# VectorE adds the scaled residual of four sublayers to the product, in place of TensorE matmuls with a scaled identity

## The chip, the cores and the metric

The kernel runs on one core of a Trainium2 chip (trn2). The metric is the device time of one execution in microseconds (us); lower is better.

## The reference

The reference is two transformer blocks over 256 tokens of width 1024, in fp32. Seven sublayers matter here, numbered 1 to 7 as `b` in the code.

```python
for i in range(DEPTH):                     # DEPTH = 2, ALPHA = (2 * DEPTH) ** 0.25
    y = mixer_i(x)                         # i = 0: short convolution, i = 1: latent attention
    x = _layer_norm(ALPHA * x + y, ln_mix_g[i], ln_mix_b[i])
    x = _layer_norm(ALPHA * x + _sq_relu_mlp(x, ff_w1[i], ff_w2[i]), ln_ff_g[i], ln_ff_b[i])
# second block
x = x + 0.5 * swiglu(rms_norm(x, ...))
x = x + hybrid_mixer(x, ...)
x = x + 0.5 * swiglu(rms_norm(x, ...))
return rms_norm(x, final_norm)
```

Sublayers 1 to 4 are the two mixers and the two MLPs of the first block: each ends in a product `y`, a residual `ALPHA * x`, and a layer norm. Sublayers 5 to 7 belong to the second block, add the residual with a factor of 0.5 or 1, and are followed by an RMS norm.

## The kernel before

**Tiling.** Tokens stand on the 128 partitions in two tiles (`TILES`), so `x_tok` is [128, 2, 1024]. Each tile is handled in two halves of 512 columns (`HALVES`). The accumulator `acc` is PSUM, [128, 4, 512]: bank `2 * tile + h` holds half `h` of tile `tile` of a sublayer's product. Four more PSUM banks, `up[0..3]`, take the products into the hidden width, the transposes and the filler matmuls.

**Weights.** SyncE loads the weights in slabs of up to 1 MB into a ring of four (`raw`). ScalarE rounds each slab to `weight_hi` (L569) and VectorE takes the rest, `weight_lo` (L933). Every product is three matmuls: high by high, high by low, low by high (L1401 to L1403 into `up`, L1434, L1435 and L1437 into `acc`).

**The end of a sublayer.** `last_products` finishes tile 0 of `acc` first, then the two halves of tile 1, and signals `acc_part` and `slab_used`. VectorE's `layer_norm` (called for b = 1 to 4) then does for each tile: statistics of both halves from `acc` (L983), their aggregation (L985), subtract and scale by the gain from `acc` into `x_tok` (L992), and multiply by the root and add the bias in `x_tok` (L997). GpSimd works out the root in between (L487, L488). The residual is already in `acc` by then.

**How the residual got there.** `carry` starts each accumulator bank with a matmul of `x_tok` by `alpha_ident`, ALPHA times the identity, in fp32 (L1507, 512 columns each; each leaves two records in the trace). Four are issued for every one of the sublayers 1 to 4: at the start of the program for the first, two in `turn` and two in `mlp_part` for each MLP, and one after each of the steps 1 to 4 of the attention for the third. For sublayers 5 and 7 the accumulator is started with `clear_acc` instead, four matmuls of a single row of zeros (L1513).

**The next sublayer's operand.** `turn` is TensorE's code between two sublayers: fillers (`keep_warm`, bf16 matmuls of zeros, L1478), transposes of tile 0 (`turn_tile`, L1489), `carry` of tile 0, fillers, transposes of tile 1. Each half of a tile is transposed when its `tok` signal comes. ScalarE copies the transposes to `xh` (L569) and VectorE takes the rest to `xl` (L933). `WARM` holds the numbers of fillers: 9 and 8 for b = 1, 4 and 3 for b = 3, 22 and 0 for b = 4. Between sublayers 2 and 3, TensorE transposes tile 0, multiplies it by the first weights of the attention (`fresh_product`, L1620, L1621, L1626), and transposes tile 1 after that; VectorE there takes the rest of tile 0 (`middle`) between the statistics and L992 of tile 1. After sublayer 4 a second norm follows, the RMS norm of the second block (squares by ScalarE, L609, and L1015 by VectorE), before the transposes.

**Order.** Every engine's order is written out by hand and kept by semaphores; nothing is scheduled by a program. The first SyncE transfer brings the constants up to `C_ANTI`, the identity and the scaled identity, 128 KB.

Of the kernel before, what the change touches and what calls it, by code (L numbers as in the profile page):

```python
# [26 lines left out]
ALU = mybir.AluOpType  # L27
AX_X = mybir.AxisListType.X

P = 128  # L30
# [4 lines left out]
HALF = 512  # L35
# [7 lines left out]
ALPHA = (2.0 * DEPTH) ** 0.25  # L43
# [25 lines left out]
ROWS = ROW_XBC_B + XT  # L69


C_ID, C_ALPHA, C_ANTI, C_TRI, C_AFTER, C_SWAP, C_COS, C_SIN = 0, 128, 256, 384, 512, 640, 768, 1024
C_ALL = 1280


def shape_constants():

    c = np.zeros((P, C_ALL), np.float32)
    i = np.arange(P)
    c[:, C_ID:C_ID + P] = np.eye(P)  # L80
    c[:, C_ALPHA:C_ALPHA + P] = ALPHA * np.eye(P)
    c[:, C_ANTI:C_ANTI + P] = np.eye(P)[::-1]
    c[:, C_TRI:C_TRI + P] = i[:, None] <= i[None, :]
    c[:, C_AFTER:C_AFTER + P] = i[:, None] > i[None, :]

    h = ROPE // 2
    for d in range(P):
        src, sign = (d + h, -1.0) if d % ROPE < h else (d - h, 1.0)
        c[src, C_SWAP + d] = sign
    inv = np.float32(10000.0) ** (-np.arange(0, ROPE, 2, dtype=np.float32) / np.float32(ROPE))  # L90
    ang = np.arange(TOKENS, dtype=np.float32)[None, :] * inv[i % h][:, None]
    c[:, C_COS:C_COS + TOKENS] = np.cos(ang)
    c[:, C_SIN:C_SIN + TOKENS] = np.sin(ang)
    return c


def two_blocks(nc, t, consts, out):
# [40 lines left out]
    with ExitStack() as ctx:  # L138
# [10 lines left out]
        x_tok = sb("x_tok", [P, TILES, D])  # L149
# [9 lines left out]
        gain = sb("gain", [P, D])  # L159
        bias = sb("bias", [P, D])  # L160
        gain2 = sb("gain2", [P, D])
        cst = sb("cst", [P, C_ALL])
        rows = sb("rows", [ROWS, P])
# [5 lines left out]
        stat = sb("stat", [P, TILES, 2, 6])  # L169
        mean_var = sb("mean_var", [P, TILES, 2])  # L170
        rstd = sb("rstd", [P, 4])
# [5 lines left out]
        acc = ctx.enter_context(nc.psum_tensor("acc", [P, 4, HALF], F32))  # L177
        up = [ctx.enter_context(nc.psum_tensor(f"up{i}", [P, HALF], F32)) for i in range(4)]

        ident = cst[:, C_ID:C_ID + P]  # L180
        alpha_ident = cst[:, C_ALPHA:C_ALPHA + P]
        anti = cst[:, C_ANTI:C_ANTI + P]
        tri = cst[:, C_TRI:C_TRI + P]
        after = cst[:, C_AFTER:C_AFTER + P]
# [71 lines left out]
                return self.s[n]  # L256

        NORMS = 8
        norm = [Sems(f"norm{b}", "rows rstd tok" + " stat" * (b <= 4) + " resid squares" * (b >= 4)) if b else None for b in range(NORMS)]

        turned, operand_high, operand_low, acc_part = (
            sem("turned"), sem("operand_high"), sem("operand_low"), sem("acc_part"))
# [658 lines left out]
        def _(dve):  # L921
            steps = [0]
            vec = nc.vector

            def then(ins):

                steps[0] += 1
                ins.then_inc(dve_step, 1)
                dve.wait_ge(dve_step, steps[0])
# [43 lines left out]
            HALVES = (slice(0, HALF), slice(HALF, D))  # L973

            def layer_norm(b, last, rows_landed, ready, middle=None):

                for tile in range(TILES):
                    x = x_tok[:, tile, :]  # L980
                    for h, c in enumerate(HALVES):
                        product_done(b, tile, h, last)
                        ins = vec.bn_stats(stat[:, tile, h, :], acc[:, 2 * tile + h, :])  # L983
                    then(ins)
                    vec.bn_aggr(mean_var[:, tile, :], stat[:, tile, :, :].rearrange("p a b -> p (a b)"))\  # L985
                        .then_inc(norm[b]["stat"], 1)
                    if tile and middle:
                        middle()
                    dve.wait_ge(norm[b]["rows"], rows_landed)
                    dve.wait_ge(norm[b]["stat"], tile + 1)  # L990
                    for h, c in enumerate(HALVES):
                        ins = vec.scalar_tensor_tensor(x[:, c], acc[:, 2 * tile + h, :], mean_var[:, tile, 0:1], gain[:, c],  # L992
                                                       ALU.subtract, ALU.mult)
                    then(ins)
                    dve.wait_ge(norm[b]["rstd"], tile + 1)
                    for c in HALVES:
                        vec.scalar_tensor_tensor(x[:, c], x[:, c], rstd[:, tile:tile + 1], bias[:, c],  # L997
                                                 ALU.mult, ALU.add).then_inc(norm[b][ready], 1)
# [242 lines left out]
            for tile in range(TILES):  # L1241
                sl = slice(tile * SSD_HEADS, (tile + 1) * SSD_HEADS)
                ins = vec.tensor_tensor(x_dt[:, sl], acc[:, 2, sl], dtb_row, ALU.add)
# [144 lines left out]
        def _(pe):  # L1388
            mm = nc.tensor.matmul
# [102 lines left out]
            def turn(b, src):  # L1492
                if b:
                    keep_warm(WARM[b][0])
                turn_tile(b, src, 0)
                if b in (1, 3):
                    carry(0)
                if b:
                    keep_warm(WARM[b][1])
                turn_tile(b, src, 1)  # L1500
                if b in (4, 6):
                    clear_acc()

            def carry(tile, halves=(0, 1)):

                for h in halves:
                    mm(acc[:, 2 * tile + h, :], alpha_ident, x_tok[:, tile, h * HALF:(h + 1) * HALF], start=True,  # L1507
                       stop=False, skip_group_check=True)

            def clear_acc():  # L1510

                for n in range(4):
                    mm(acc[:, n, :], zeros[0:1, 0:P], zeros[0:1, :], start=True, stop=False, skip_group_check=True)  # L1513
# [5 lines left out]
            keep_warm(8)  # L1519
            pe.wait_ge(ident_landed, 16)  # L1520
            turn(0, x_tok)
            carry(0)
            carry(1)


            m = S_SC
# [27 lines left out]
            def mlp_part(i, b):  # L1554
                s, q = S_FF[i], mlp[i]
                weights(s)
                carry(1, (0,))
                up_product(s, up[0], b - 1)
                carry(1, (1,))
                with pe.Fori(0, FF_CHUNKS // 2 - 1) as it:  # L1560
                    for j in range(4):
                        m = s + 1 + j
                        weights(m, 4 * it)
                        if j % 2 == 0:
                            up_product(m, up[(1, 0)[j // 2]])
                        else:
                            pe.wait_ge(q["chunk"], 2 * it + (1 + j // 2))
                            down_product(m, *hidden(j // 2), CT)
                m = s + N_FF - 3
                weights(m)  # L1570
                up_product(m, up[1])
                last_products(b, CT, [(m + 1, *hidden(0), lambda: pe.wait_ge(q["chunk"], FF_CHUNKS - 1)),
                                      (m + 2, *hidden(1), lambda: pe.wait_ge(q["chunk"], FF_CHUNKS))])
# [193 lines left out]
                down_product(WO + c, *latent_rows(c), CT)  # L1767

            for g in range(HEADS + 1):
                if g == 1:  # L1770
                    step(g, values_ready)
                elif g in (6, 7):
                    step(g, lambda: first_rows(g - 6))
                else:
                    step(g)
                if 1 <= g <= 4:
                    carry((g - 1) // 2, ((g - 1) % 2,))
            last_products(3, CT, [(WO + c, *latent_rows(c), lambda c=c: heads_out(c)) for c in (2, 3)])

            turn(3, x_tok)  # L1780
# [181 lines left out]
```

## Time and profile before

| | |
|---|---|
| median of 3 runs | 1182.96 us (1181.51 to 1185.43) |
| span of the profiled execution | 1181.9 us (its own run time is not listed apart from the three) |
| PE (TensorE matmul) busy | 1162.1 us, 98% |
| PEld (TensorE weight load) busy | 1041.8 us |
| DVE (VectorE) busy | 658.0 us, 56% |
| ACT (ScalarE) busy | 514.1 us, 43% |
| POOL (GpSimd) busy | 51.0 us, 4% |
| mean granted TensorE clock | 0.993 |

A profile is one execution. Its times are in us, durations marked ns are the mean of one instruction. The chain of waits follows the work that ended last back through whatever released it. "PEclk" is the clock that TensorE was granted, 1.00 for 2.4 GHz and 0.50 for 1.2 GHz.

### The profile page before, as it was taken

Reading aid. Unit: us, or ns where it says so; the run is one execution under the profiler, and the core shown is the slowest. Engines: PE = TensorE matmul, PEld = TensorE weight load, DVE = VectorE, ACT = ScalarE, POOL = GpSimd, SP = SyncE. Lnnn points to the kernel's source line nnn. Section 1 sums busy time; section 2 is a strip of 40 time slices with the busy share of each in tenths; the row PEclk is TensorE's granted clock in tenths of the full one; section 3 lists DMA queues with packets and bytes.
Section 4 is the critical chain, followed back from the end, with each engine's and each line's share of the span. In section 5 each row is a group of like instructions: output and inputs, shape, how many; then the busy total and the mean of one; then the engine's idle time right before and its main releaser. Section 6 shows DMA issues by size and latency. Waiting matters only on the chain.

```text
span 1181.9 us, 18506 instructions
## 1 busy us (share of the span) xinstructions
PE 1162.1 (98%) x7660; PEld 1041.8 (88%) x7668; DVE 658.0 (56%) x717; ACT 514.1 (43%) x581; POOL 51.0 (4%) x93
## 2 busy tenths in 40 slices
PE   9999999999999999999999999999999999999997
PEld 7997999998977799999889999989988878999996
DVE  4757554555654755545654544467854565544543
ACT  4433444443544344444344443445635644434342
POOL 1000000000200100000000000010120010000000
PEclk9999999999999999999999999998989999999999
DMA  9664656554641565565346555556651144456541
GB/s 338 220 211 146 213 178 197 182 180 120 211 161 36 177 219 179 190 183 187 127 144 213 178 177 177 198 156 202 192 164 37 37 161 139 149 181 206 189 148 54
DMA packets 140908, 199.67 MB, mean 169 GB/s; under 512 B 9240, under 2 KB 119024, under 8 KB 140864
## 3 DMA queue, kind: packets, MB, share of 16 engines
q1 hardware_dynamic: 138160, 190.27, 50.0%
q0 software_dynamic: 2704, 8.79, 2.4%
q8 instruction: 32, 0.52, 0.2%
q14 instruction: 12, 0.10, 0.0%
HBM read 197.99 MB, written 1.05 MB: 168 GB/s over the span
## 4 chain that ended last, share of the span: by engine, by line
PE 92%; DVE 3%; ACT 2%; DMA 2%; POOL 1%; issue 1%; SPq 0%; DVEq 0%; POOLq 0%; ACTq 0%
PE up L1401 15%; PE up L1403 15%; PE up L1402 15%; PE acc L1434 11%; PE acc L1435 11%; PE acc L1437 11%; DMA raw<-in_sc_w_in 2%; PE acc L1507 1%; PE up L1489 1%; PE up L1850 1%; PE up L1876 1%; PE up L1478 1%; PE up L1873 1%; PE up L1743 1%; PE up L1423 1%; PE up L1427 1%
## 5 line engine op out<-in xcount | busy, mean ns | idle before, releaser
L933 DVE TENSOR_TENSOR weight_lo<-raw,weight_hi 128x2048 fp32r<-128x2048 f32 (+3 forms) x206 | 414.4, 2017 | 312.4 <-ACT weight_hi L569 312.2
L1401 PE MATMUL up<-xh,weight_hi 128*128 128x256 f32 x1548 | 441.3, 285 | 1.9 <-ACT cols L569 0.8
L569 ACT ACTIVATE weight_hi<-raw 128x2048 fp32r<-128x2048 f32 (+3 forms) x206 | 347.3, 1693 | 213.6 <-PE acc L1437 119.7
L1402 PE MATMUL up<-xl,weight_hi 128*128 128x256 f32 x1548 | 438.9, 283 | 0.0
L1403 PE MATMUL up<-xh,weight_lo 128*128 128x256 f32 x1548 | 438.8, 283 | 0.0
L1401 PEld LDWEIGHTS up<-xh,weight_hi 128*128 128x128 f32 x1548 | 297.8, 192 | 5.9 <-issue 1.7
L1402 PEld LDWEIGHTS up<-xl,weight_hi 128*128 128x128 f32 x1548 | 297.9, 192 | 2.7 <-issue 0.7
L1403 PEld LDWEIGHTS up<-xh,weight_lo 128*128 128x128 f32 x1548 | 297.7, 192 | 0.0
L1434 PE MATMUL acc<-weight_hi,hh 128*128 128x512 f32 x480 | 187.6, 391 | 0.6 <-DVE hl L933 0.4
L1435 PE MATMUL acc<-weight_lo,hh 128*128 128x512 f32 x480 | 187.5, 391 | 0.0
L1437 PE MATMUL acc<-weight_hi,hl 128*128 128x512 f32 x480 | 150.3, 389 | 0.0
L1437 PEld LDWEIGHTS acc<-weight_hi,hl 128*128 128x128 f32 x480 | 90.1, 188 | 19.1
L1434 PEld LDWEIGHTS acc<-weight_hi,hh 128*128 128x128 f32 x480 | 90.3, 188 | 18.8 <-issue 1.9
L1435 PEld LDWEIGHTS acc<-weight_lo,hh 128*128 128x128 f32 x480 | 90.3, 188 | 17.0
L656 ACT ACTIVATE tmp_a<-up 128x512 f32<-128x512 f32 x32 | 19.1, 598 | 120.7 <-PE up L1403 115.9
L1074 DVE TENSOR_TENSOR tmp_b<-tmp_a 128x512 f32<-128x512 f32 x32 | 22.2, 693 | 65.5 <-ACT tmp_a L656 65.5
L1434 PE MATMUL acc<-weight_hi,xh 128*128 128x256 f32 (+2 forms) x168 | 55.8, 332 | 1.3 <-DVE xl L933 1.3
L692 ACT ACTIVATE tmp_a<-up 128x512 f32<-128x512 f32 x22 | 13.1, 597 | 97.3 <-PE up L1403 93.2
L1435 PE MATMUL acc<-weight_lo,xh 128*128 128x256 f32 (+2 forms) x168 | 55.2, 329 | 0.0
L1437 PE MATMUL acc<-weight_hi,xl 128*128 128x256 f32 (+2 forms) x168 | 50.6, 328 | 0.0
L569 ACT ACTIVATE xh<-up 128x512 fp32r<-128x512 f32 (+1 forms) x43 | 22.7, 551 | 55.2 <-PE up L1489 43.0
L933 DVE TENSOR_TENSOR xl<-up,xh 128x512 fp32r<-128x512 f32 (+1 forms) x43 | 25.2, 629 | 27.5 <-ACT xh L569 27.3
(215 smaller groups left out, 892.7 us busy)
## 6 DMA issues: line engine op xcount, KB each, us to landing
raw<-in_ff_w SPq DMA_DIRECT2D x64, 1024.0 KB, 5.7
raw<-in_ffn_w_gate SPq DMA_DIRECT2D x22, 1024.0 KB, 5.3
raw<-in_ffn_w_up SPq DMA_DIRECT2D x22, 1024.0 KB, 5.4
raw<-in_ffn_w_down SPq DMA_DIRECT2D x44, 512.0 KB, 4.7
raw<-in_w_in SPq DMA_DIRECT2D x16, 1024.0 KB, 5.7
raw<-in_sc_w_in SPq DMA_DIRECT2D x11, 1024.0 KB, 7.3
raw<-in_w_out SPq DMA_DIRECT2D x6, 1024.0 KB, 5.0
raw<-in_sc_w_out SPq DMA_DIRECT2D x4, 1024.0 KB, 5.3
```

Of the source, the lines that this page charges most:

```text
L569: return nc.scalar.activation(dst, src, ACT.Copy, **kw)
L656: nc.scalar.activation(tmp_a[:, :], up[par][:, :], ACT.Relu).then_inc(q["relu"], 1)
L692: nc.scalar.activation(tmp_a[:, :], up[2 * par][:, :], ACT.Silu).then_inc(q["gate"], 1)
L933: return vec.tensor_tensor(dst, whole, high.bitcast(F32), ALU.subtract)
L1074: vec.tensor_tensor(tmp_b[:, :], tmp_a[:, :], tmp_a[:, :], ALU.mult).then_inc(q["squared"], 1)
L1401: mm(dst, w_h, xh[:, x_tile + k, :], start=first and k == 0, stop=False)
L1402: mm(dst, w_h, xl[:, x_tile + k, :], start=False, stop=False)
L1403: ins = mm(dst, w_l, xh[:, x_tile + k, :], start=False, stop=last and k == k_tiles - 1)
L1423: mm(dst, w_h[k], xh[:, k, :], start=k == 0, stop=False)
L1434: mm(d, s_h, h, start=first, stop=False, **open_group)
L1435: mm(d, s_h, l, start=False, stop=False, **open_group)
L1437: ins = mm(d, s_l, h, start=False, stop=last, **open_group)
```

## The change

TensorE no longer puts the residual into `acc`. All `carry` calls and the scaled identity are gone; `clear_acc` starts the banks in their place, once for each sublayer: at the start of the program, at the end of `turn` for b = 1 and 3, and before step 2 of the attention. VectorE's `layer_norm` first adds: for each half, `x_tok = ALPHA * x_tok + acc`, and then takes the statistics and the subtraction from `x_tok`. Two waits on VectorE's own sum precede the statistics. The constants shrink by 128 columns, all of them in the first transfer.

```diff
-C_ID, C_ALPHA, C_ANTI, C_TRI, C_AFTER, C_SWAP, C_COS, C_SIN = 0, 128, 256, 384, 512, 640, 768, 1024
-C_ALL = 1280
+C_ID, C_ANTI, C_TRI, C_AFTER, C_SWAP, C_COS, C_SIN = 0, 128, 256, 384, 512, 640, 896
+C_ALL = 1152
...
                     for h, c in enumerate(HALVES):
                         product_done(b, tile, h, last)
-                        ins = vec.bn_stats(stat[:, tile, h, :], acc[:, 2 * tile + h, :])
-                    then(ins)
+                        vec.scalar_tensor_tensor(x[:, c], x[:, c], ALPHA, acc[:, 2 * tile + h, :], ALU.mult, ALU.add)\
+                            .then_inc(norm[b]["sum"], 1)
+                        if h:
+                            dve.wait_ge(norm[b]["sum"], 2 * tile + 1)
+                            vec.bn_stats(stat[:, tile, 0, :], x[:, HALVES[0]])
+                    dve.wait_ge(norm[b]["sum"], 2 * tile + 2)
+                    then(vec.bn_stats(stat[:, tile, 1, :], x[:, HALVES[1]]))
...
-                        ins = vec.scalar_tensor_tensor(x[:, c], acc[:, 2 * tile + h, :], mean_var[:, tile, 0:1], gain[:, c],
+                        ins = vec.scalar_tensor_tensor(x[:, c], x[:, c], mean_var[:, tile, 0:1], gain[:, c],
...
                 turn_tile(b, src, 0)
-                if b in (1, 3):
-                    carry(0)
                 if b:
                     keep_warm(WARM[b][1])
                 turn_tile(b, src, 1)
-                if b in (4, 6):
+                if b in (1, 3, 4, 6):
                     clear_acc()
-
-            def carry(tile, halves=(0, 1)):
-
-                for h in halves:
-                    mm(acc[:, 2 * tile + h, :], alpha_ident, x_tok[:, tile, h * HALF:(h + 1) * HALF], start=True,
-                       stop=False, skip_group_check=True)
...
             turn(0, x_tok)
-            carry(0)
-            carry(1)
+            clear_acc()
...
                 weights(s)
-                carry(1, (0,))
                 up_product(s, up[0], b - 1)
-                carry(1, (1,))
...
             for g in range(HEADS + 1):
+                if g == 2:
+                    clear_acc()
...
                     step(g)
-                if 1 <= g <= 4:
-                    carry((g - 1) // 2, ((g - 1) % 2,))
```

The order of VectorE's instructions at the end of sublayer 1, before (tile 0, then the head of tile 1):

```order
L933 TENSOR_TENSOR weight_lo<-raw,weight_hi 128x2048
L983 BN_STATS stat<-acc 128x6 x2
L985 BN_AGGR mean_var<-stat 128x2
L992 SCALAR_TENSOR_TENSOR x_tok<-acc,mean_var,gain 128x512 x2
L997 SCALAR_TENSOR_TENSOR x_tok<-x_tok,rstd,bias 128x512 x2
```

And with the change:

```order
L931 TENSOR_TENSOR weight_lo<-raw,weight_hi 128x2048
L981 SCALAR_TENSOR_TENSOR x_tok<-x_tok,acc 128x512 x2
L985 BN_STATS stat<-x_tok 128x6
L987 BN_STATS stat<-x_tok 128x6
L988 BN_AGGR mean_var<-stat 128x2
L995 SCALAR_TENSOR_TENSOR x_tok<-x_tok,mean_var,gain 128x512 x2
L1000 SCALAR_TENSOR_TENSOR x_tok<-x_tok,rstd,bias 128x512 x2
```

Two instructions of 512 columns stand ahead of the statistics of each tile, and nothing has left VectorE. The same holds for both tiles of each of the four sublayers.

The order of TensorE's instructions between sublayers 1 and 2, before:

```order
L1437 MATMUL acc<-weight_hi,hl 128x512
L1478 MATMUL up<-zeros 128x512 x9
L1489 MATMUL up<-cst,x_tok 128x128 x8
L1507 MATMUL acc<-x_tok,cst 128x512 x2
L1478 MATMUL up<-zeros 128x512 x8
L1489 MATMUL up<-cst,x_tok 128x128 x8
L1507 MATMUL acc<-x_tok,cst 128x512
```

And with the change:

```order
L1440 MATMUL acc<-weight_hi,hl 128x512
L1481 MATMUL up<-zeros 128x512 x9
L1492 MATMUL up<-cst,x_tok 128x128 x8
L1481 MATMUL up<-zeros 128x512 x8
L1492 MATMUL up<-cst,x_tok 128x128 x8
L1508 MATMUL acc<-zeros 128x512 x4
```

The two carries between the tiles are gone with nothing put in their place, and the number of fillers is what it was. The carry after the second transposes has become four clears. The fourth carry, 33 rows further on behind the first product of the MLP, is gone too.

TensorE in the attention, at the end of step 1 (L1722 and L1723 are the outputs of head 0, L1714 the transposes of step 2), before:

```order
L1706 MATMUL up<-mask_ones,mask_row 128x64
L1722 MATMUL up<-prob_t,normed 128x256
L1723 MATMUL up<-prob_t,normed 128x128
L1507 MATMUL acc<-x_tok,cst 128x512
L1714 MATMUL up<-cst,arena 128x128 x3
```

And with the change:

```order
L1698 MATMUL up<-mask_ones,mask_row 128x64
L1714 MATMUL up<-prob_t,normed 128x256
L1715 MATMUL up<-prob_t,normed 128x128
L1508 MATMUL acc<-zeros 128x512 x4
L1706 MATMUL up<-cst,arena 128x128 x3
```

One carry has become four clears here; the three carries at the ends of steps 2, 3 and 4 are gone.

## Rows read from the trace of the kernel before

**Rows 1.** The page: the span, and the chain of waits by engine.

```profile
span 1181.9 us, 18506 instructions
...
PE 92%; DVE 3%; ACT 2%; DMA 2%; POOL 1%; issue 1%; SPq 0%; DVEq 0%; POOLq 0%; ACTq 0%
```

**Rows 2.** Chain of waits in time: start, us, what; sublayer 1 to 2, then 4 to 5.

```profile
108.07 0.87 PE up L1489 x8
108.94 1.72 PE acc L1507 x4
110.66 1.73 PE up L1478 x8
...
113.26 0.86 PE acc L1507 x2
...
119.87 0.86 PE acc L1507 x2
...
595.68 0.96 PE acc L1513 x4
```

**Rows 3.** Timeline of VectorE, sublayer 1 to 2: start, us, engine, line, what, count.

```profile
106.64 1.41 DVE L997 SCALAR_TENSOR_TENSOR x_tok<-x_tok,rstd,bias 128x512 f32<-128x512 f32 x2
...
111.06 1.42 DVE L997 SCALAR_TENSOR_TENSOR x_tok<-x_tok,rstd,bias 128x512 f32<-128x512 f32 x2
```

**Rows 4.** Timeline of VectorE, the residual of sublayer 5.

```profile
780.92 2.05 DVE L1006 SCALAR_TENSOR_TENSOR x_tok<-acc,x_tok 128x512 f32<-128x512 f32 x3 [1.14 <-PE acc L1437]
```

**Rows 5.** Groups by line, VectorE: count, then busy us, mean ns, idle before.

```profile
L997 DVE SCALAR_TENSOR_TENSOR x_tok<-x_tok,rstd,bias 128x512 f32<-128x512 f32 x16 | 11.3, 749 | 0.3
...
L992 DVE SCALAR_TENSOR_TENSOR x_tok<-acc,mean_var,gain 128x512 f32<-128x512 f32 x16 | 11.3, 746 | 0.7
```

**Rows 6.** Timeline, sublayer 3 to 4: VectorE's last pair, TensorE's wait for it.

```profile
403.50 1.42 DVE L997 SCALAR_TENSOR_TENSOR x_tok<-x_tok,rstd,bias 128x512 f32<-128x512 f32 x2
...
404.31 0.42 PEld L1489 LDWEIGHTS up<-cst,x_tok 128*128 128x128 f32 x4 [0.41 <-DVE x_tok L997]
```

**Rows 7.** Timeline, sublayer 2 to 3.

```profile
294.94 0.70 DVE L983 BATCH_NORM_STATS2 stat<-acc 128x6 f32<-128x512 f32 x1 [0.33 <-PE acc L1437]
...
298.65 1.42 DVE L997 SCALAR_TENSOR_TENSOR x_tok<-x_tok,rstd,bias 128x512 f32<-128x512 f32 x2
...
300.30 1.03 PE L1489 MATMUL up<-cst,x_tok 128*128 128x128 f32 x8
```

**Rows 8.** Timeline, sublayer 4 to 5.

```profile
587.27 0.70 DVE L983 BATCH_NORM_STATS2 stat<-acc 128x6 f32<-128x512 f32 x1 [0.16 <-PE acc L1437]
587.30 4.70 PE L1478 MATMUL up<-zeros 128*128 128x512 bf16 x21
...
594.36 1.32 PE L1489 MATMUL up<-cst,normed 128*128 128x128 f32 x8 [1.14 <-DVE normed L1015]
```

**Rows 9.** Chain of waits in time, attention: the carry after step 3, then steps 5 and 6.

```profile
366.12 0.86 PE acc L1507 x2
...
371.17 0.33 PE up L1714 x3
...
374.50 0.33 PE up L1714 x3
```

**Rows 10.** Timeline of ScalarE, the first stage.

```profile
29.52 1.91 ACT L569 ACTIVATE weight_hi<-raw 128x2048 fp32r<-128x2048 f32 x1 [0.60 <-DMA raw<-in_sc_w_in]
```

**Rows 11.** Windows: us; busy of PE, PEld, DVE, ACT, POOL; PEclk; DMA share, GB/s.

```profile
593.00:594.00 1.00, 0.22 (x2) 0.00 (x0) 0.45 (x1) 0.78 (x2) 0.52 (x1) 1.00 0.00 0
799.00:803.00 4.00, 4.00 (x36) 3.88 (x34) 0.32 (x1) 3.23 (x4) 0.00 (x0) 1.00 0.91 307
...
804.00:810.00 6.00, 6.00 (x29) 6.00 (x29) 3.73 (x7) 3.87 (x5) 0.00 (x0) 0.50 0.64 183
...
871.00:875.00 4.00, 3.22 (x19) 2.28 (x19) 1.29 (x2) 2.40 (x2) 0.00 (x0) 1.00 0.57 228
...
876.00:882.00 6.00, 6.00 (x25) 5.00 (x25) 2.37 (x8) 1.06 (x5) 0.00 (x0) 0.50 0.48 175
```

More of the change, by code:

```diff
@@ L80, in shape_constants @@
     c[:, C_ID:C_ID + P] = np.eye(P)
-    c[:, C_ALPHA:C_ALPHA + P] = ALPHA * np.eye(P)
     c[:, C_ANTI:C_ANTI + P] = np.eye(P)[::-1]
@@ L180, in two_blocks @@
         ident = cst[:, C_ID:C_ID + P]
-        alpha_ident = cst[:, C_ALPHA:C_ALPHA + P]
         anti = cst[:, C_ANTI:C_ANTI + P]
@@ L258, in two_blocks @@
         NORMS = 8
-        norm = [Sems(f"norm{b}", "rows rstd tok" + " stat" * (b <= 4) + " resid squares" * (b >= 4)) if b else None for b in range(NORMS)]
+        norm = [Sems(f"norm{b}", "rows rstd tok" + " stat sum" * (b <= 4) + " resid squares" * (b >= 4)) if b else None for b in range(NORMS)]
         turned, operand_high, operand_low, acc_part = (
```

## The prediction

> **What bounds the kernel.** I first read the page. The span is 1181.9 us and TensorE makes up 92% of the chain of waits, VectorE 3% [rows 1]. So time that leaves TensorE is time won, but only where TensorE is what the chain runs through, and the change moves work exactly at the places where it may not be: the ends of sublayers. So I read the chain in order of time around them, then both engines' timelines, then the windows for the clock.
>
> Between sublayers 1 and 2 the chain stays on TensorE: transposes of tile 0, two carries of 0.86 us each, eight fillers of 1.73 us, then tile 1 from 112.39, a carry, and another carry at 119.87 [rows 2]. That looks like pure TensorE time. But fillers do no work; they stand there because TensorE would wait. The other side of the wait is VectorE: its last pair for tile 0 runs from 106.64 to 108.05, and for tile 1 from 111.06 to 112.48, each instruction 0.71 us [rows 3]. The first half of tile 1 is ready at 111.77, only 0.62 us before TensorE takes it up. Between 3 and 4, with three fillers in place of eight, TensorE already waits for VectorE (0.41 us at 404.31) [rows 6]. **At the end of a sublayer VectorE is the limit, or within 0.6 us of it**, and what sits on TensorE there between the tiles is cover.
>
> **What VectorE gains in work.** Two instructions per tile, `x_tok = ALPHA * x_tok + acc`. The nearest row has the same operands and form: three residual adds from `acc` take 2.05 us end to end, 0.68 each [rows 4]; the pairs of L997 give 0.71 [rows 3]. Two are 1.37 to 1.42, and the two waits for its own sum may add up to 0.1 each, since the second add runs while the first statistics wait for nothing. Bounds for a tile are 1.37 to 1.6; I take 1.4, next to the row of the same form, and 2.8 for both tiles. Nothing hides it: VectorE works tile 0 and tile 1 back to back.
>
> The statistics and L992 now read SBUF instead of PSUM. The trace has the pair to compare: L997 reads SBUF in 749 ns, L992 reads `acc` in 746 [rows 5]. I price that part of the edit at nothing. The Trainium skill (VectorE: DVE Perf Modes, section on the TRN2 errata) gives a VectorE instruction a shorter fixed part from SBUF than from PSUM, 58 against 120 cycles at 0.96 GHz, which by an estimate from that page takes 0.26 us off each tile and 2.1 us off the whole sum. The rows here do not show it.
>
> **Sublayer 1 to 2.** Tile 1's first half comes at 111.77 + 2.8 = 114.57, and TensorE, which started at 112.39, starts 2.2 later. The second half is late by 0.7 more, where before both were there or nearly: TensorE ends the transposes at 112.48 + 2.8 + 0.47 = 115.75 against 113.26 [rows 2, 3], 2.5 later. Then come four clears, 0.96 us [rows 2], in place of one carry, 0.86: +0.1. The carry at 119.87 goes: -0.86. The two carries between the tiles, 1.72 us, save nothing: TensorE waits there instead. Sum **+1.7**.
>
> **Sublayer 3 to 4.** VectorE is already waited for, so all of 2.8 counts; +0.1 and -0.86 as before. Sum **+2.0**.
>
> **Sublayer 2 to 3.** Before tile 1's statistics VectorE idles 0.33 us for the product [rows 7], which the adds fill; its tokens come 2.8 - 0.33 = 2.5 later, at 301.8 and 302.5 instead of up to 300.07. TensorE is kept busy by the first product of tile 0 until 300.46, so it waits 1.4 from there on for the half that counts for the product behind [rows 7]. Tile 0 does not matter: its first half is ready at 294.7, when TensorE comes to it. Sum **+1.4**. No carry stands here.
>
> **Sublayer 4 to 5.** VectorE idles 0.16 us before the last statistics [rows 8]; then everything behind it, the second norm included, waits on it, and TensorE waits for the result already (1.14 us at 594.36). 2.8 - 0.16 = **+2.6**, with nothing removed.
>
> **Attention.** Four carries of 0.86 go, four clears of 0.96 in all come: -2.5. Is TensorE the limit? A step with a carry takes 4.19 us, and step 5, the first without, takes 374.50 - 371.17 = 3.33 with no wait in the chain [rows 9]: 4.19 - 0.86 to the last digit. So the whole of it is won: **-2.5**. Bounds: -2.5, and -1.9 if the chain of softmax becomes the limit in the middle steps.
>
> **Start.** Four carries become clears, but in the first stage ScalarE waits for weights up to 29.52 [rows 10], behind TensorE's gain. The first transfer loses 64 KB of 128. I take -0.1, between 0 and -0.3.
>
> Sum: 1.7 + 2.0 + 1.4 + 2.6 - 2.5 - 0.1 = **+5.1 us**. Against the profiled execution that is a span of 1187.0; the median lies 1.06 above that span, so 1188.1 for the median.
>
> **The clock.** The carries between the tiles also kept TensorE busy. Without them it idles: from the first token of tile 0 to that of tile 1, VectorE takes 111.06 - 106.64 + 1.4 = 5.8 us, of which transposes and their wait are 1.15. With eight fillers of 0.216 (1.73 us) that leaves 2.95 us idle after sublayer 1, with three (0.65) 4.0 us after sublayer 3. After sublayer 4 the fillers from 587.30 end at 592.0 [rows 8] and tile 0 comes 2.6 later than now: 2.5 us, then 1.1 again. The longest such wait at the end of these sublayers now is 1.14 us [rows 8]. Where TensorE did little, the clock fell to 1.2 GHz and stayed there about 6.8 us: after 3.9 us of 16-column matmuls (0.50 from 804 to 810) and after a gap of 0.8 us with narrow matmuls behind it (0.50 from 876 to 882). It did not fall around 593 to 594, where TensorE was 0.22 us busy in one [rows 11]. The new gaps are longer than that and fall between the two kinds. The Trainium skill (TensorE: Matmul & The Clock Gate, Part 1) says that the throttled clock is the default and activity releases it; the rows above agree. The same page (Part 4) says that transposes do not count as activity; the transposes on both sides of 593 to 594 with the clock at 1.00 speak against that.
>
> Price of one fall: 6.8 us at half clock costs between 0 (all of it idle) and 3.4. Part of it lies in the wait that caused it, and I take half, 1.7. Three falls give 5.1, so 1188.1 + 5.1 = **1193.2**.
>
> **The rivals.**
> *Tail alone.* The clock holds, or falls once at most in idle time: 1188.1, up to 1190. For it: the stretch around 593. Against: gaps of 3 to 4 us. Chance 0.27.
> *Falls in the attention too.* Without carries its steps hold only narrow matmuls, as 871 to 875 did [rows 11]. One more fall there, all on TensorE's path, costs 3.4: 1196.6. Against: steps 5 on run so today at full clock. Chance 0.10.
> *TensorE is the limit after all (faster).* If VectorE's adds were hidden, the 12 carries behind the start would all be won, 12 x 0.86 = 10.3, less three groups of clears, 2.9: -7.4, or 1175.5. It decides at 112.39: tile 1's first half would have to be ready then, and by the sum it comes 2.2 us later; VectorE has no idle stretch there to hide two adds per tile in. Chance 0.05.
> *Reads from SBUF are shorter.* The two statistics and the two L992 of a tile change their source. If each became shorter by what lies between the slow and the fast kind of this instruction in the rows, 0.75 and 0.68 us [rows 4, 5], a tile would win 0.27 and the four sublayers 2.2, so the sum would be 5.1 - 2.2 = 2.9: 1185.9 with the clock held. L997 against L992 speaks against it [rows 5]. Chance 0.06. This is the errata section named above at work.
> *The change does not do what it says.* Excluded by the order shown: the adds are there and the carries are not.
>
> **The numbers.** The forecast of two or three falls has 0.52. About 0.3%, 3.5 us, is what a measurement of this kernel can tell from no change: 1179.4 to 1186.5. Faster is the third rival, 0.05. Same is the fourth, and a little of the first with adds at their lower bound: 0.10. Slower is the rest, 0.85. The range runs from 1187, the tail alone at its lower bounds, to 1199, the forecast with each fall near 3.4; it leaves out the rivals three and four and some of the second.
>
> **What would show it.** The adds at 0.68 to 0.75 us, two per tile, and `x_tok` of tile 1 2.8 us later after 1 and 3; TensorE waiting for L1000 before the second transposes, about 3 us after sublayer 1 and 4 after sublayer 3, where 0.41 is the longest of these two now; PEclk below 1.00 in the windows behind these gaps, and a mean clock of about 0.985 in place of 0.993; steps 1 to 4 of the attention at 3.33 us, with one clear group. I am wrong if TensorE's waits at the four places together are under 5 us, if the windows behind them stay at 1.00, or if the adds take well under 0.6 us.

## The result, and the profile after

| | before | changed kernel |
|---|---|---|
| median | 1183.51 us (1181.51 to 1185.43) | 1198.81 us (1197.10 to 1200.81) |
| ratio to before | | 1.013, 95% interval 1.0113 to 1.0147 |
| span of the profiled execution | 1181.9 us | 1198.8 us (its run took 1200.81) |
| mean granted TensorE clock in that span | 0.993 | 0.978 (0.980 to 0.983 in the other runs) |

The change makes the kernel 1.3% slower, 15.3 us. The forecast was 1193.2 with a range from 1187 to 1199: the sign is right and the range just holds the median, but the forecast itself is 5.6 us short. A second timing of the same kernel, `x9_after_again` below, gives 12.2 us, ratio 1.0109 (1.0089 to 1.0129); of the 3.1 us between the two, 1.7 lie in the kernel before (1183.51 here, 1185.21 there). The profiled run is the slowest of four, so the sums below, made in its trace, come out some 2 us above the median's.

The page of the changed kernel: span, busy time, and the chain by engine, which answers to [rows 1].

```profile
span 1198.8 us, 18498 instructions
...
PE 1169.5 (98%) x7652; PEld 1049.6 (88%) x7652; DVE 667.0 (56%) x733; ACT 514.0 (43%) x581; POOL 54.4 (5%) x93
...
PE 89%; DVE 6%; ACT 2%; POOL 1%; issue 1%; DMA 0%; DVEq 0%; POOLq 0%; SPq 0%; ACTq 0%
```

TensorE lost the carries and is busy 7.4 us longer than before. VectorE's share of the chain doubles from 3% to 6%. The table of waits (TensorE, what it waited for, us in all, times, longest) says where:

```profile
PE up L1492 <- DVE x_tok L1000: 7.5, 4, 3.6
PE up L1492 <- DVE normed L1018: 3.5, 3, 2.6
```

VectorE's timeline between sublayers 1 and 2 (start, us, line, what), which answers to [rows 3]:

```profile
105.25 1.28 DVE L981 SCALAR_TENSOR_TENSOR x_tok<-x_tok,acc 128x512 f32<-128x512 f32 x2
106.44 0.69 DVE L985 BATCH_NORM_STATS2 stat<-x_tok 128x6 f32<-128x512 f32 x1
107.04 0.68 DVE L987 BATCH_NORM_STATS2 stat<-x_tok 128x6 f32<-128x512 f32 x1
107.75 0.21 DVE L988 BATCH_NORM_AGGREGATE mean_var<-stat 128x2 f32<-128x12 f32 x1
108.09 1.42 DVE L995 SCALAR_TENSOR_TENSOR x_tok<-x_tok,mean_var,gain 128x512 f32<-128x512 f32 x2
109.54 1.41 DVE L1000 SCALAR_TENSOR_TENSOR x_tok<-x_tok,rstd,bias 128x512 f32<-128x512 f32 x2
...
115.15 1.42 DVE L1000 SCALAR_TENSOR_TENSOR x_tok<-x_tok,rstd,bias 128x512 f32<-128x512 f32 x2
```

The pair of adds stands at 105.25 and the statistics at 106.44, so a tile pays 1.19 us for them. From one L1000 pair to the next it is 115.15 - 109.54 = 5.61, where before it was 111.06 - 106.64 = 4.42 [rows 3]: the same 1.19. TensorE in the same stretch, and behind sublayers 3 and 4 (in brackets the idle time before, and its releaser):

```profile
107.60 2.12 PE L1481 MATMUL up<-zeros 128*128 128x512 bf16 x9
110.34 1.32 PE L1492 MATMUL up<-cst,x_tok 128*128 128x128 f32 x8 [0.63 <-DVE x_tok L1000]
111.50 1.89 PE L1481 MATMUL up<-zeros 128*128 128x512 bf16 x8
115.96 1.96 PE L1492 MATMUL up<-cst,x_tok 128*128 128x128 f32 x8 [2.57 <-DVE x_tok L1000]
...
411.60 1.32 PE L1492 MATMUL up<-cst,x_tok 128*128 128x128 f32 x8 [3.64 <-DVE x_tok L1000]
...
604.38 1.97 PE L1492 MATMUL up<-cst,normed 128*128 128x128 f32 x8 [2.58 <-DVE normed L1018]
```

These are the idle stretches that the prediction named: 2.95, 4.0 and 2.5 us were forecast, 2.57, 3.64 and 2.58 came. In the windows behind them, and in two more (at the start and at 1004), the granted clock is at its lower level (us; busy of PE, PEld, DVE, ACT, POOL with the number of instructions; PEclk; DMA share, GB/s):

```profile
10.00:17.00 7.00, 5.77 (x27) 5.80 (x28) 4.36 (x3) 3.31 (x3) 3.46 (x6) 0.51 1.09 358
119.00:122.80 3.80, 3.80 (x16) 3.14 (x15) 2.69 (x3) 3.15 (x2) 0.00 (x0) 0.50 0.63 210
...
413.00:419.00 6.00, 6.00 (x24) 4.68 (x23) 5.21 (x5) 4.16 (x3) 1.17 (x3) 0.50 0.85 267
...
605.00:614.00 9.00, 8.79 (x36) 6.66 (x35) 6.98 (x8) 7.21 (x7) 1.81 (x4) 0.50 0.39 120
1004.00:1006.50 2.50, 2.50 (x13) 2.50 (x13) 1.72 (x2) 2.50 (x2) 0.00 (x0) 0.50 0.34 129
```

TensorE has its lower level, 1.2 GHz, in all of them, and it is **busy** in nearly all of each: 3.80 of 3.80, 6.00 of 6.00, 8.79 of 9.00. In these places the trace before had no fall. It has two in the second block, at 804 and 876 [rows 11], and one in the last 3 us of the program; all three are there after the change as well, and no table below counts the last one, which costs nothing. The granted clock in the trace of the changed kernel gives the lengths: 6.8 us from 10.2 (behind a wait for `weight_lo`), 6.8 from 116.0, 6.8 from 413.0, 10.2 from 604.1 and 3.4 from 1003.5.

In the attention the carries are gone, and TensorE has no wait that it did not have before (one of 1.0 us in both). The chain in time, the step with the clears and the next:

```profile
364.94 0.96 PE acc L1508 x4
365.90 0.48 PE up L1706 x3
...
369.38 0.33 PE up L1706 x3
...
372.71 0.33 PE up L1706 x3
```

The step with the clears in front takes 3.48 us and the next ones 3.33, as forecast. So TensorE's saving there is real, 2.3 us in place of the 2.5 forecast, and the loss is elsewhere: at the turns, and in falls at the start and at 1003.5.

**Where the time went.** The span cut at the end of each sublayer's product, where TensorE's fillers or transposes begin, and for the attention at the 12 fillers ahead of its steps (so "1 to 2" runs from the end of sublayer 1's product to that of sublayer 2's); changed kernel less before, in the profiled executions:

| stretch | us |
|---|---|
| start to the end of sublayer 1 | +1.6 |
| 1 to 2 | +4.7 |
| 2 to 3 | +0.9 |
| attention | -2.3 |
| 3 to 4 | +4.9 |
| 4 to 5 | +5.7 |
| 5 to 6 | -0.1 |
| 6 to the end | +1.5 |
| sum | +16.9 |

The prediction has 1.7, 1.4, -2.5, 2.0 and 2.6 for the five stretches in the middle, -0.1 for the start, and 5.1 for falls. Its terms for the tails (the ends of sublayers, where VectorE's norm is waited for) can be right only if each fall costs about 3 us. The experiments separate the two.

### The profile page after: what moved, and what is told of

It reads as the page before. It is cut to its first block, busy times and chain, and to the rows that moved or that the text cites. A ratio compares the mean times of both kernels' runs of the same rounds, so it can differ in the third digit from the quotient of the medians.

```text
span 1198.8 us, 18498 instructions
## 1 busy us (share of the span) xinstructions
PE 1169.5 (98%) x7652; PEld 1049.6 (88%) x7652; DVE 667.0 (56%) x733; ACT 514.0 (43%) x581; POOL 54.4 (5%) x93
## 3 DMA queue, kind: packets, MB, share of 16 engines
q0 software_dynamic: 2704, 8.79, 2.4%
## 4 chain that ended last, share of the span: by engine, by line
PE 89%; DVE 6%; ACT 2%; POOL 1%; issue 1%; DMA 0%; DVEq 0%; POOLq 0%; SPq 0%; ACTq 0%
PE up L1404 15%; PE up L1406 15%; PE up L1405 15%; PE acc L1437 10%; PE acc L1438 10%; PE acc L1440 10%; PE up L1426 1%; PE up L1427 1%; DVE weight_lo L931 1%; DVE x_tok L995 1%; PE up L1430 1%; PE up L1492 1%; PE up L1842 1%; DVE x_tok L981 1%; PE up L1868 1%
## 5 line engine op out<-in xcount | busy, mean ns | idle before, releaser
L1438 PEld LDWEIGHTS acc<-weight_lo,hh 128*128 128x128 f32 x480 | 90.3, 188 | 16.9
```

Source lines behind the costliest of these rows:

```text
L1438: mm(d, s_h, l, start=False, stop=False, **open_group)
```

## The experiments

All runs were timed beside the kernel before on the same chip (medians 1185.12, 1185.37 and 1185.21 in the three jobs).

**Fillers in every new wait.** `x1_fill_all` keeps the change and fills TensorE's idle stretches.

```diff
...
-            WARM = {1: (9, 8), 3: (4, 3), 4: (22, 0), 5: (6, 7), 6: (7, 2)}
+            WARM = {1: (11, 19), 3: (4, 19), 4: (33, 0), 5: (6, 7), 6: (7, 2)}
...
             turn(0, x_tok)
             clear_acc()
+            for n in range(9):
+                mm(acc[:, n % 4, :], zeros[:, 0:P], zeros[:, :], start=False, stop=False, skip_group_check=True)
```

> The changed kernel with more zero fillers where TensorE now idles: 9 after the first clears, 11 and 19 in place of 9 and 8 between sublayers 1 and 2, 19 in place of 3 between 3 and 4, 33 in place of 22 after sublayer 4. Theory A (most of the loss is the clock that falls in the new idle stretches, and a fall costs up to 3.4 us because TensorE is the limit right behind the wait): the clock is back near 0.993 and the time falls by 10 to 13 us, to 1186 to 1189. Theory B (the loss is VectorE's longer tail, and the clock costs little since it falls in waits): no change, 1197 to 1200.

Measured: 1191.0 us median, ratio 1.0056 (1.0038 to 1.0074), mean clock 0.990 to 0.994. TensorE's timeline and a window of it, behind sublayer 3:

```profile
403.48 4.26 PE L1481 MATMUL up<-zeros 128*128 128x512 bf16 x19
407.94 1.32 PE L1492 MATMUL up<-cst,x_tok 128*128 128x128 f32 x8 [0.19 <-DVE x_tok L1000]
```

```profile
404.00:408.00 4.00, 3.81 (x19) 1.55 (x18) 3.81 (x8) 0.28 (x1) 1.12 (x2) 1.00 0.00 0
```

TensorE still gets tile 1 when VectorE has it, but at 1.00. With nothing but matmuls of zeros 15.3 us (12.2 in the second timing) becomes 5.9, so half to three fifths of the loss are gone. That is less than theory A's 10 to 13 us, and the time lies between the ranges of both theories: theory A put too much on the clock. What is left is VectorE's longer tail. The profile is of the fastest of the four runs (1187.76 us at 0.994; the others ran at 0.990 or 0.991).

**The adds alone.** `x2_adds_only` is the kernel before with the new `layer_norm`, its factor 0.0 in place of ALPHA, since the carries stay.

```diff
...
-                        ins = vec.bn_stats(stat[:, tile, h, :], acc[:, 2 * tile + h, :])
-                    then(ins)
+                        vec.scalar_tensor_tensor(x[:, c], x[:, c], 0.0, acc[:, 2 * tile + h, :], ALU.mult, ALU.add)\
+                            .then_inc(norm[b]["sum"], 1)
...
```

> The kernel before with VectorE's new instructions alone: it adds with a factor of 0 what the carries have already put into the accumulator, so the residual comes from TensorE and only VectorE's work and its waits are new. By the spacing of 1.2 us per tile that the changed kernel shows, the tail alone gives 1.8 + 0.9 + 2.4 + 2.3 = 7.4 us, 1191. Theory A: the carries still fill part of the waits, so the clock falls after sublayer 4, perhaps after 3, and not after 1: 1191 to 1197, clock 0.984 to 0.993. Theory B: the tail is the whole loss, and here the 5 us that TensorE saved in the changed kernel are missing too: 1203 or more.

Measured: 1193.83 us, ratio 1.008 (1.0062 to 1.0098), clock 0.990 to 0.993. Timeline of TensorE behind sublayer 3, where the carries still stand between the tiles:

```profile
405.41 1.88 PE L1512 MATMUL acc<-x_tok,cst 128*128 128x512 f32 x4
407.13 0.81 PE L1483 MATMUL up<-zeros 128*128 128x512 bf16 x3
409.87 1.32 PE L1494 MATMUL up<-cst,x_tok 128*128 128x128 f32 x8 [1.93 <-DVE x_tok L1002]
```

The wait is 1.93 in place of 3.64, and no new fall comes anywhere; theory A expected one after sublayer 4. The four ends of sublayers grow by 2.3, 0.9, 2.4 and 2.4, 8.0 in all, of the 9.5 us that eight tiles' adds take at 1.19 each: nearly all of VectorE's work is on the path.

**TensorE's part alone.** `x3_tensor_only` is the changed kernel with the `layer_norm` of before: clears and no carries, and no adds on VectorE. It leaves out the residual of sublayers 1 to 4.

```diff
...
-                        vec.scalar_tensor_tensor(x[:, c], x[:, c], ALPHA, acc[:, 2 * tile + h, :], ALU.mult, ALU.add)\
-                            .then_inc(norm[b]["sum"], 1)
...
+                        ins = vec.bn_stats(stat[:, tile, h, :], acc[:, 2 * tile + h, :])
+                    then(ins)
...
```

> The changed kernel with the layer norm of the kernel before: the residual of sublayers 1 to 4 is left out, and only TensorE's part of the change is made. It gives what the removed carries are worth where VectorE's tail is unchanged: 0.6 + 0.8 between 1 and 2, 0.8 between 3 and 4, 2.3 in the attention, so 4.5 us, 1179; about 1.4 less if the clock falls at the start for want of the carries. Theory A and B agree on the carries; A adds that the clock falls at the start here too.

Measured: 1185.39 us, ratio 1.0004 (0.9991 to 1.0016), clock 0.984 to 0.991. Windows of it:

```profile
404.50:407.50 3.00, 3.00 (x15) 3.00 (x15) 2.21 (x2) 3.00 (x2) 0.07 (x1) 0.50 0.98 298
596.00:598.50 2.50, 2.50 (x14) 2.50 (x14) 1.72 (x1) 2.50 (x2) 0.00 (x0) 0.50 1.00 331
```

Even with no work added anywhere, taking TensorE's carries away gains nothing that can be measured; 4.5 us were expected. The attention is 2.3 us shorter as expected. 1 to 2 is only 0.6 shorter and not 1.4: tile 1's transposes start 0.4 us earlier and then wait for each half. The clock takes the rest back: the start is 0.6 longer, 3 to 4 is 1.0 longer and 4 to 5 1.5 longer, with a fall of 3.4 us in each of the three. The fall behind sublayer 4 (595.3) follows the wait of 1.14 us that the kernel before has too, at full clock [rows 8, 11]. Behind sublayer 3 it falls after a wait of 1.64 us, where x2, waiting 1.93, held it. The ten runs go from 1182.21 us at 0.991 to 1188.37 at 0.984, 0.9 us for each 0.001. Nor do the two halves add up: x2 gives +8.7 and x3 +0.3, together +9.0, and the whole change +15.3, or +12.2 in the second timing. The rest appears only when the longer wait and the missing cover meet.

**Fillers at the turns only, at the start only, after sublayer 4 only.** `x6_fill_turns` is x1's WARM without the start, `x5_fill_start` the nine fillers at the start alone, `x8_fill_4` this:

```diff
...
-            WARM = {1: (9, 8), 3: (4, 3), 4: (22, 0), 5: (6, 7), 6: (7, 2)}
+            WARM = {1: (9, 8), 3: (4, 3), 4: (33, 0), 5: (6, 7), 6: (7, 2)}
```

`x9_after_again` is the changed kernel once more, beside x8.

> The changed kernel with more fillers in the waits of TensorE behind sublayers 1, 3 and 4 (WARM 11 and 19, 4 and 19, 33 and 0 in place of 9 and 8, 4 and 3, 22 and 0), nothing else. The question is what the three falls there cost. Theory A (3.0 to 3.4 us a fall, since each begins when VectorE's tile 1 comes and TensorE is the limit behind it): 1.00 from 115 to 123, 412 to 420 and 603 to 614, the intervals 1 to 2, 3 to 4 and 4 to 5 shorter by 3 us each, and 9 to 10 us faster than the changed kernel, about 1189 to 1190. Theory B (1.7 us a fall, as predicted): 5 us faster, about 1193 to 1194. Theory C (the waits cost, not the clock): no fall, yet under 2 us faster. The fall at the start stays in all of them.

> The changed kernel with nine fillers of zeros behind the first four clears, nothing else. The question is what the fall of the clock at the start costs (0.50 from about 10 to 17 us, behind a wait of 2.12 us for weight_lo). Theory A (a fall costs about 3 us because it begins when the wait ends and TensorE is the limit from there): the window from 10 to 17 shows 1.00 and the kernel is 0.6 to 1.4 us faster than the changed kernel, less than 3 because in this stage TensorE waits for weights again before 30 us; everything from 106 us on is shifted and otherwise as in the changed kernel. Theory B (falls are priced by their length alone, 3.4 us each): 3 us or more faster. Theory C (the clock follows what TensorE did over a longer stretch): the fall after sublayer 1 goes as well, and it is 4 us or more faster.

> The changed kernel with the fillers behind sublayer 4 raised from 22 to 33, nothing else: one of the three places of the run with 11, 19 and 33 fillers, by itself. Theory A (each fall has its own price of 3.0 to 3.4 us, since TensorE is the limit behind each wait): the fall at 603 (10.2 us long in the changed kernel) goes or shrinks, the interval 4 to 5 is 3 us shorter, the falls behind 1 and 3 stay, and the kernel is 3 us faster than the changed kernel in the same job. Theory B (the three places were worth 9 us only together, since the clock remembers earlier idle time): under 1.5 us. Theory C (fillers past the wait delay the transposes): slower.

> The changed kernel again, unedited, as the measure for the other edits on this chip. All theories: 13 to 16 us slower than the kernel before, ratio 1.011 to 1.015, falls of the clock behind sublayers 1, 3 and 4; their lengths, 3.4 to 10.2 us, may differ from the first profile of it.

Measured, with every stretch less the same stretch of the kernel before, and in brackets the length of the fall in it (none: 0):

| kernel | median, ratio | start | 1 to 2 | 3 to 4 | 4 to 5 | 6 to end |
|---|---|---|---|---|---|---|
| x1 | 1191.0, 1.0056 | +0.9 (0) | +1.8 (0) | +1.9 (0) | +2.4 (0) | 0.0 (0) |
| x6 | 1189.98, 1.0040 | +1.1 (3.4) | +1.8 (0) | +1.9 (0) | +3.9 (3.4) | +1.5 (3.4) |
| x5 | 1200.88, 1.0142 | +0.1 (0) | +3.3 (3.4) | +4.9 (6.8) | +5.7 (10.2) | +1.5 (3.4) |
| x7, below | 1199.80, 1.0129 | +1.4 (3.4) | +3.2 (3.4) | +5.6 (10.2) | +5.5 (10.2) | +1.5 (3.4) |
| x8 | 1196.76, 1.0095 | +0.3 (0) | +4.8 (6.8) | +5.5 (10.2) | +2.4 (0) | 0.0 (0) |
| x9 | 1197.44, 1.0109 | +1.2 (6.8) | +4.7 (6.8) | +4.9 (6.8) | +2.7 (3.4) | 0.0 (0) |
| changed | 1198.81, 1.0130 | +1.6 (6.8) | +4.7 (6.8) | +4.9 (6.8) | +5.7 (10.2) | +1.5 (3.4) |

The stretches left out are alike in all seven, but for 5 to 6 in x1: it is 1.8 us shorter there, because its first fall in the second block has 3.4 us in place of 6.8.

Read down a column and the price of a fall stands there. 1 to 2: 1.8 without, 3.3 with 3.4 us, 4.7 with 6.8. 3 to 4: 1.9, then 4.9 with 6.8, 5.5 or 5.6 with 10.2. 4 to 5: 2.4, then 2.7 or 3.9 with 3.4, and 5.7 with 10.2. **A fall of 6.8 us costs 2.9 to 3.0**, close to the 3.4 that half a clock can cost at most (an estimate: half of 6.8). Longer ones add less, 3.2 to 3.7 for 10.2, since some of their length lies in waits. What 3.4 us cost depends on where they lie. In x9 the fall begins with tile 0's transposes behind sublayer 4 and costs 0.3: TensorE waits again before tile 1, and the slower transposes only eat up that wait. Timeline of TensorE in x9, then in x8, which has no fall there:

```profile
603.93 1.97 PE L1492 MATMUL up<-cst,normed 128*128 128x128 f32 x8 [2.58 <-DVE normed L1018]
606.11 1.59 PE L1492 MATMUL up<-cst,normed 128*128 128x128 f32 x8 [0.21 <-DVE normed L1018]
```

```profile
605.96 1.32 PE L1492 MATMUL up<-cst,normed 128*128 128x128 f32 x8 [0.86 <-DVE normed L1018]
```

In x6 the fall begins at 602.7, behind both waits, and costs 1.5.

The fillers at the turns are worth 1198.81 - 1189.98 = 8.8 us against the first timing and 7.5 against x9: short of the 9 to 10 that my theory gave, above the 5 of the rival. Falls do not come alike in each run: x6's profile has one left at 602.7, and x9's has only 3.4 us behind sublayer 4. So x8 has no fall there, as my theory wants it (4 to 5 at +2.4), but against x9 that saves only 0.3 us in the traces. Its median lies 0.7 us under that of x9, not 3, and the two intervals overlap (1.0079 to 1.0112, and 1.0089 to 1.0129): as a timing it is inconclusive. x9 itself came out 12.2 us slower than before, a little under the 13 to 16 expected. Nothing was gained at the start, where 0.6 to 1.4 us were expected: x5 is no faster than the changed kernel, and x1 no faster than x6. In the traces with this layer norm the start is 1.1 to 1.6 us longer than before with a fall in it and 0.1 to 0.9 without; the medians do not show it.

**The sum back into PSUM.** `x7_sum_in_acc` writes it over `acc`, so that the statistics and L995 read PSUM.

```diff
...
-                        vec.scalar_tensor_tensor(x[:, c], x[:, c], ALPHA, acc[:, 2 * tile + h, :], ALU.mult, ALU.add)\
+                        vec.scalar_tensor_tensor(acc[:, 2 * tile + h, :], x[:, c], ALPHA, acc[:, 2 * tile + h, :], ALU.mult, ALU.add)\
...
```

> The changed kernel with the sum written back into acc instead of x_tok, so that the statistics and the subtraction read PSUM as in the kernel before; the adds, the clears and the fillers stay. Theory A (VectorE's reads of SBUF hold up GpSimd, whose power takes 0.90 us beside them in place of 0.57, and VectorE's own instructions are no shorter from SBUF): the power is back at 0.57 us, rstd comes 0.3 us earlier, the statistics take 0.64 to 0.70 again in place of 0.60 spacing, and the time is within 1 us of the changed kernel, most of a gain in 4 to 5, where VectorE waits 0.46 and 0.77 us for rstd. Theory B (the source of the reads matters for VectorE: 58 against 120 cycles would be 0.26 us a tile): the tails are 2 us longer in all and the kernel is 2 us slower. Theory C (where the power takes its time doesn't depend on VectorE's operands): the power stays at 0.90.

Measured: 1199.8 us, ratio 1.0129 (1.0104 to 1.0153): no change. Timeline of VectorE in it, tile 0 of sublayer 1:

```profile
104.99 1.29 DVE L981 SCALAR_TENSOR_TENSOR acc<-x_tok,acc 128x512 f32<-128x512 f32 x2
106.18 0.69 DVE L985 BATCH_NORM_STATS2 stat<-acc 128x6 f32<-128x512 f32 x1
106.79 0.68 DVE L987 BATCH_NORM_STATS2 stat<-acc 128x6 f32<-128x512 f32 x1
107.51 0.21 DVE L988 BATCH_NORM_AGGREGATE mean_var<-stat 128x2 f32<-128x12 f32 x1
```

The spacings are those of the changed kernel within 0.02 us: 1.19, 0.61, 0.72 against 1.19, 0.60, 0.71. (I had expected the statistics 0.64 to 0.70 apart; they are not.) Whether these instructions read SBUF or PSUM makes no difference to VectorE. It matters to GpSimd, told below.

**Carries as cover.** `x4_carry_for_fill` goes back to the kernel before and takes up what the change gained. The attention begins with 12 fillers; three of its four carries take their place and the fourth goes before step 1, so none lengthens a later step.

```diff
-            keep_warm(12)
...
+            values_ready()
+            carry(0)
+            carry(1, (0,))
...
-                    step(g, values_ready)
+                    carry(1, (1,))
+                    step(g)
...
-                if 1 <= g <= 4:
-                    carry((g - 1) // 2, ((g - 1) % 2,))
```

> The kernel before with three of the attention's four carries in the place of its 12 fillers (2.5 us), and the fourth at the start of step 1. If TensorE is the limit in the steps, three carries of 0.86 us go off the path and nothing comes on to it: -2.6 us, 1181. If the softmax is the limit behind the fillers, no change.

Measured: 1182.18 us, ratio 0.9983 (0.9972 to 0.9993), clock 0.990 to 0.995. Its timeline, start of the attention:

```profile
348.80 2.84 PE L1507 MATMUL acc<-x_tok,cst 128*128 128x512 f32 x6
...
354.05 1.13 PE L1507 MATMUL acc<-x_tok,cst 128*128 128x512 f32 x2
```

The attention is 2.3 us shorter than before, the same 2.3 that the change gives, with no work moved to VectorE. The median is 2.9 us under the kernel before, the fastest of all the kernels here, though by less than the 0.3% that I called measurable; its interval lies under 1. Its profiled run is 4.0 us shorter than that of before; 1.5 of that is the clock of the second block, with one fall of 10.2 us at 800 in place of the two of 6.8, and no part of the edit.

## Why the prediction was right, and where it was short

**The bound, and the sign: right.** "At the end of a sublayer VectorE is the limit, or within 0.6 us of it." x2 shows it: with TensorE's work unchanged, four ends are longer by 8.0 us. That also rules out the rival that TensorE is the limit after all, which needed the adds to be hidden. x3 agrees from the other side: with 1.72 us of carries gone from between the tiles, tile 1's transposes start only 0.4 us earlier.

**The adds: over-sized, harmless.** 1.4 us a tile was forecast from the busy time of a pair. The pair's busy time came out at 1.28, and even that counts the last one's end, which overlaps the next instruction; from start to start it is 1.19 us. So 2 to 3 came to 0.9 and not 1.4, and 4 to 5 to 2.4 and not 2.6.

**The tail: right.** With no fall in them (x1) the five middle stretches are +1.8, +0.9, -2.3, +1.9, +2.4, in all +4.6, where the prediction has 1.7 + 1.4 - 2.5 + 2.0 + 2.6 = +5.2. The 1.8 of 1 to 2 is reached with smaller adds, for two reasons: tile 1's transposes now wait for each half, 1.25 us to the clears in place of 0.87, and VectorE was nearer than the 0.62 us read from the rows (x3 gains 0.4 by it). "TensorE waits there instead" of the two carries between the tiles holds.

**The idle stretches and the three falls: right.** All three places came, and the two rivals beside it did not. *Tail alone* was to be 5.1 us over before; x1, which is that case made, is 5.9 over, and the change is 15.3 or 12.2. *Falls in the attention too*: no trace has a fall in the attention's steps.

**The price of a fall: the step that failed.** "Part of it lies in the wait that caused it, and I take half, 1.7." It does not lie in that wait. The windows above show the wait at full clock and the fall behind it, mostly over work that is on TensorE's path (behind sublayer 4 a second, shorter wait takes some of it up, as x9 shows): 598 to 604, with the wait in it, is still at 1.00, and 605 to 614 is at 0.50:

```profile
598.00:604.00 6.00, 3.79 (x18) 1.53 (x16) 5.36 (x10) 1.64 (x6) 3.12 (x6) 1.00 0.00 0
```

The prediction had 3.4 as the bound for work on the path and used it for the attention; for the tails it should have stood as well. Against x1's stretches the three falls cost 2.9, 3.0 and 3.3 us, 9.2 for the 5.1 forecast; with three at 3.0, 1188.1 + 9.0 = 1197.1. The profiled executions then add up: 4.6 for the tails and the attention, 9.2 for the three falls, 1.6 at the start and 1.5 behind sublayer 6 make the 16.9. That the range still holds the median is partly luck: its upper end stood for three falls near 3.4, and the falls outside the three places came on top.

**Falls outside the three places: missed.** The profiled run has one more at the start, where the prediction had -0.1 and +1.6 came, and one at 1003.5, and a length of 10.2 where 6.8 was taken. The one at 1003.5 is behind a piece of code that the change leaves alone, with a wait of 0.71 us where before had 0.72 at full clock:

```profile
1001.10 1.32 PE L1492 MATMUL up<-cst,normed 128*128 128x128 f32 x8 [0.71 <-DVE normed L1018]
```

All eleven traces of this study have that wait (0.71 or 0.72 us); the fall behind it is in four of them (the changed kernel, x5, x6, x7) and costs 1.5 us each time. The second trace of the changed kernel, x9, does not have it, so it comes with the run, and the median holds only part of it. Whether the change makes it more frequent is not shown: it stands in four of the seven traces of the changed kernel and the variants with its new waits or fillers, and in none of the other four (before, x2, x3, x4).

**Reads from SBUF: the rival is gone.** The Trainium skill (VectorE: DVE Perf Modes, the section on the TRN2 errata) gives VectorE a shorter fixed part from SBUF than from PSUM. In x7 the four instructions of a tile that read the sum read it from PSUM instead, and the two adds write it there; no spacing differs by more than 0.02 us from the changed kernel's, so for these fp32 instructions of 512 columns the measurement decides against it.

## What to carry to other kernels

Before moving work off the busiest engine, look whether the place is one where it waits: there its "work" cost next to nothing here (0.4 of 1.72 us), and the added work on the engine that it waits for cost nearly all of its time (8.0 of 9.5 us). Matmuls in such a wait also held the clock for what comes behind. Price a fall at about half of that part of its length that lies over work on the path (3.0 us for 6.8), and look for a further wait behind it that takes some of it up (0.3 us for 3.4 in x9). Where a kernel has both useful off-path matmuls and fillers, put the first in the place of the second: that was worth 2.3 us here.

## What the runs showed that I had not expected

**GpSimd is slower beside VectorE.** The root of the variance on GpSimd (L486) takes 0.90 us in the changed kernel and 0.57 in x7. Timelines of GpSimd, sublayer 1, first the changed kernel, then x7:

```profile
108.37 0.90 POOL L486 TENSOR_TENSOR rstd<-rstd,half_neg 128x1 f32<-128x1 f32 x1
```

```profile
108.12 0.57 POOL L486 TENSOR_TENSOR rstd<-rstd,half_neg 128x1 f32<-128x1 f32 x1
```

Beside it VectorE runs L995, with both tensors in SBUF (`x_tok`, `gain`) in the first and one of them in PSUM in the second; of what runs beside it x7 changes only that. The Trainium skill ("SBUF — State Buffer", section "SBUF: two separate sides") says that VectorE, in an instruction with two SBUF inputs, and a GpSimd instruction that reads SBUF exclude each other at a pair of ports, and that the later one waits. The two traces agree that GpSimd is held up, by 0.33 us. It costs nothing at most places, since L1000 starts behind L995 anyway; only behind sublayer 4, where the second norm waits for the root, does x7's stretch come out 0.1 to 0.2 us shorter (5.5 against 5.7 with the same fall).

**Falls vary between runs of one kernel.** The changed kernel's two profiles have 10.2 and 3.4 us behind sublayer 4, and only the first has the fall at 1003.5. The five traces with the same waits behind sublayers 1 and 3 (changed kernel, x5, x7, x8, x9) have falls of 3.4 to 6.8 us behind the first and of 6.8 to 10.2 behind the second. Time follows the clock: the kernel before ran in 1182.0 us at 0.994 and 1186.8 at 0.990, 1.2 us for 0.001. A wait alone does not decide: 1.93 us with carries ahead of it held the clock (x2), 1.64 with three fillers ahead lost it (x3). The same wait of 1.14 us behind sublayer 4 held it in the kernel before and lost it in x3. What does decide was not settled.
